# One input projection of a two-layer hybrid backbone: z and q computed in pieces of two row blocks by 512 columns

## The chip, the cores and the metric

The kernel runs on one core of one Trainium2 chip. TensorE (PE) multiplies, ScalarE (ACT), VectorE (DVE) and GpSimd (POOL) do the rest, SyncE (SP) issues the large loads; each takes its own instructions in order, and semaphores tie them together. The metric is the device time of one execution in microseconds. The kernel before took 1467.08 us (median of three runs, 1463.37 to 1467.37).

## The reference, cut to what matters

Two layers work on 256 latent tokens and 256 context tokens of 1024 features. Each layer projects the normed tokens by one matrix `w_in` and cuts the columns apart: k and v, x and B and dt of a state-space scan, C, q (512 columns), z (512 columns), and 1536 for a long convolution. z gates the scan, q goes into attention:

```python
h = _modulate(_rmsnorm(x, p['norm1_g']), sh1, sc1)
proj = h @ p['w_in']                                   # 1024 x 3856
...
q = _rope2d(_rmsnorm(_split_heads(proj[..., OFF_Q:OFF_Q + ATTN_INNER], ATTN_HEADS), p['q_norm_g']), rope) * ATTN_SCALE
...
y = y * jax.nn.silu(z.astype(F32))                     # z = proj[..., OFF_Z:OFF_Z + SSD_INNER]
y = _rmsnorm(y, p['ssd_norm_g'])
```

In the second layer (the last) the context tokens need neither z nor q, so these are computed for 256 tokens there and for 512 in the first.

## The kernel before, in words

Every product with a weight is computed as three float32r matmuls: high part of h by high part of w, high by low, low by high. The weights come in pieces of 128 partitions x 1024 numbers (512 KB) into a ring of four slots. A piece goes SP (load to `w_raw`), ACT (`round_w`, L1165, makes `w_hi`), DVE (`split_w`, L1467, makes `w_lo` over `w_raw`), PE. PE raises `w_used` when it is done with a piece, and SP waits for it before it loads the piece that is four further on into the same slot.

The projection takes 30 pieces per layer, in fifteen chunks of 256 columns and two pieces each (rows 0 to 511 of w_in, then 512 to 1023; the table `W_IN`). The order is four chunks `xbc` (pieces 0 to 7), two of `z` (8 to 11), `kv` (12, 13), two of `q` (14 to 17), six of `hy` (18 to 29). In the text "piece 8" is s = 8 of this count, in either layer.

Chunks xbc and hy are turned (features on partitions, moving operand h, up to 512 tokens wide, L595 to L597). Chunks z, kv and q have tokens on partitions: the stationary operand is a 128 x 128 block of h, the moving operand 256 columns of weights (L865 to L867). For each tile of 128 tokens PE runs through all eight blocks of rows, 24 matmuls, and so through both pieces; a tile takes half a PSUM bank. PE waits for both split pieces ahead of the first tile, and gives back both in the last tile: the first piece 12 matmuls before the second.

PSUM has eight banks. Banks 0 to 3 are two pairs, which chunks take in turn (`q % 2` of a running count, "pair 0" and "pair 1" here). `pair_open` makes PE wait until the pair's last reader has raised `pair_free`. z is read by ACT (Silu into `zs`, L1229), q by DVE (copy into `qk`, L1592), one chunk each, two tiles to an instruction. The other banks carry small work that is put between the pieces by hand: `at_piece(s)` ahead of a piece and `in_piece(s)` in its middle. There stand the spectra of the convolution's filter in layer 0 (`filter_spectrum`, L689, at pieces 9 to 11, copied by DVE at L1643), the scan (`cum_rows` L716 and L719, ACT's exponentials L1284, `y_head` L731; L823, L829), and the modulation rows of layer 0 (L534, L554). What ACT and DVE do in slot s is written out in the same way in two loops over s, in the order of their lines.

## Time and profile before

| what | value |
|---|---|
| three runs | 1467.37, 1467.08, 1463.37 us |
| the profiled execution | 1465.52 us, span 1463.7 us |
| granted TensorE clock over the span | 0.969 |
| PE busy | 1355.6 us (93%) |
| DVE busy, ACT busy | 695.9 us (48%), 525.1 us (36%) |
| projection of layer 0 | about 65 to 325 us of the span |
| projection of layer 1 | about 969 to 1124 us of the span |

The span runs from the first instruction to the last; 1.8 us of the profiled execution lie around it. The duration of a matmul in the rows holds its way through the array, so matmuls overlap; what one costs in a stream is read from start to start. In a timeline row the first number is the start, the second the time, and the bracket is how long the engine had been idle and what ended that.

### The profile page before, as it was taken

The page shows a single profiled execution, that of the slowest core. Times are in us where ns is not written, and L with a number is a line of the kernel's source. Part 1 is how long each engine was busy: PE and PEld are TensorE (multiplying, and loading weights), DVE is VectorE, ACT ScalarE, POOL GpSimd, SP SyncE. Part 2 cuts the span into 40 slices and gives each one's busy share as a digit, 9 for nine tenths or more (in the row PEclk, how much of TensorE's full clock was granted, in tenths as well). Part 3 has the DMA queues.
Part 4 walks back from the last instruction along what each step waited for, and adds up shares of the span by engine and source line. Part 5 has one row for each costly group of instructions (what it writes and reads, how often), then busy time and mean ns, then how long its engine had stood idle before and what let it go on. Part 6 is the DMA issues. An engine that isn't in the chain of part 4 may idle for free. (4 is left out here: it accounts for less than half of the span.)

```text
span 1463.7 us, 20023 instructions
## 1 busy us (share of the span) xinstructions
PE 1355.6 (93%) x8564; PEld 1093.0 (75%) x8564; DVE 695.9 (48%) x1134; ACT 525.1 (36%) x866; POOL 1.7 (0%) x8
## 2 busy tenths in 40 slices
PE   4799999998989889999999999999987889899997
PEld 2376778776657667777777788659876768899996
DVE  0544244755556663433222233364486555655554
ACT  4443333643031352222112232355464224544442
POOL 0000000000000000000000000000000000000000
PEclk9699999999999999999999999999999999999998
DMA  9553313442101215545555533313333203465652
GB/s 296 163 144 86 116 58 120 121 139 97 43 1 30 73 51 176 173 148 169 164 163 165 169 116 93 94 29 110 92 87 101 73 15 87 130 184 178 185 175 85
DMA packets 171216, 172.03 MB, mean 118 GB/s; under 512 B 9172, under 2 KB 169590, under 8 KB 171128
## 3 DMA queue, kind: packets, MB, share of 16 engines
q1 hardware_dynamic: 169284, 170.41, 38.2%
q8 instruction: 67, 1.10, 0.3%
q10 hardware_dynamic: 1844, 0.36, 0.1%
q14 instruction: 21, 0.17, 0.0%
HBM read 169.69 MB, written 1.05 MB: 117 GB/s over the span
## 5 line engine op out<-in xcount | busy, mean ns | idle before, releaser
L1467 DVE TENSOR_TENSOR w_lo<-w_raw,w_hi 128x1024 fp32r<-128x1024 f32 (+1 forms) x220 | 264.0, 1203 | 312.2 <-ACT w_hi L1165 311.4
L1165 ACT ACTIVATE w_hi<-w_raw 128x1024 fp32r<-128x1024 f32 (+1 forms) x220 | 228.3, 1042 | 396.6 <-DMA w_raw<-in_w_gu_dram 183.7
L595 PE MATMUL ps<-h_hi,w_hi 128*128 128x512 f32 (+1 forms) x960 | 340.0, 354 | 3.1 <-DVE w_lo L1467 2.5
L596 PE MATMUL ps<-h_lo,w_hi 128*128 128x512 f32 (+1 forms) x960 | 330.6, 344 | 0.0
L597 PE MATMUL ps<-h_hi,w_lo 128*128 128x512 f32 (+1 forms) x960 | 330.5, 344 | 0.0
L595 PEld LDWEIGHTS ps<-h_hi,w_hi 128*128 128x128 f32 x960 | 183.9, 192 | 43.0 <-issue 20.6
L595 PE MATMUL ps<-f_hi,w_hi 128*128 128x512 f32 (+1 forms) x544 | 191.2, 352 | 14.9 <-DVE xT L1773 5.3
L597 PEld LDWEIGHTS ps<-h_hi,w_lo 128*128 128x128 f32 x960 | 183.6, 191 | 22.2
L596 PEld LDWEIGHTS ps<-h_lo,w_hi 128*128 128x128 f32 x960 | 183.9, 192 | 19.5
L597 PE MATMUL ps<-f_hi,w_lo 128*128 128x512 f32 (+1 forms) x544 | 184.7, 339 | 0.0
L596 PE MATMUL ps<-f_lo,w_hi 128*128 128x512 f32 (+1 forms) x416 | 141.2, 340 | 0.0
L595 PEld LDWEIGHTS ps<-f_hi,w_hi 128*128 128x128 f32 x544 | 104.4, 192 | 33.3 <-issue 12.0
L597 PEld LDWEIGHTS ps<-f_hi,w_lo 128*128 128x128 f32 x544 | 104.6, 192 | 11.2
L596 PEld LDWEIGHTS ps<-f_lo,w_hi 128*128 128x128 f32 x416 | 80.2, 193 | 9.0 <-issue 1.0
L865 PE MATMUL ps<-w_hi,h_hi 128*128 128x256 f32 x256 | 77.6, 303 | 0.0
L866 PE MATMUL ps<-w_lo,h_hi 128*128 128x256 f32 x256 | 74.0, 289 | 0.0
L867 PE MATMUL ps<-w_hi,h_lo 128*128 128x256 f32 x256 | 73.9, 289 | 0.0
L865 PEld LDWEIGHTS ps<-w_hi,h_hi 128*128 128x128 f32 x256 | 50.7, 198 | 4.6 <-issue 4.4
L1330 ACT ACTIVATE probT<-ps 128x512 f32<-128x512 f32 (+1 forms) x48 | 22.6, 523 | 87.3 <-PE ps L944 87.3
L1502 DVE SCALAR_TENSOR_TENSOR xT<-ps,modv,xT 128x256 f32<-128x256 f32 x72 | 30.4, 477 | 48.6 <-PE ps L597 48.5
L866 PEld LDWEIGHTS ps<-w_lo,h_hi 128*128 128x128 f32 x256 | 50.8, 198 | 0.4 <-issue 0.2
L867 PEld LDWEIGHTS ps<-w_hi,h_lo 128*128 128x128 f32 x256 | 50.7, 198 | 0.0
(276 smaller groups left out, 1605.6 us busy)
## 6 DMA issues: line engine op xcount, KB each, us to landing
w_raw<-in_w_gu_dram SPq DMA_DIRECT2D x88, 512.0 KB, 3.6
w_raw<-in_w_in_dram SPq DMA_DIRECT2D x60, 512.0 KB, 4.1
w_raw<-in_w_down_dram SPq DMA_DIRECT2D x32, 512.0 KB, 3.4
m_raw<-in_w_mod_dram SPq DMA_DIRECT2D x30, 512.0 KB, 5.2
m_even<-in_w_mod_dram SPq DMA_DIRECT2D x13, 1024.0 KB, 6.2
m_odd<-in_w_mod_dram SPq DMA_DIRECT2D x12, 1024.0 KB, 6.3
m_first<-in_w_mod_dram SPq DMA_DIRECT2D x8, 1024.0 KB, 13.2
w_raw<-in_w_out_dram SPq DMA_DIRECT2D x16, 512.0 KB, 3.4
```

Source lines behind the costliest of these rows:

```text
L595: mm(o, w_hi[:, i % RING, w], hi[:, 0:n], start=first and k == 0, stop=False)
L596: mm(o, w_hi[:, i % RING, w], lo[:, 0:n], start=False, stop=False)
L597: last = mm(o, w_lo[:, i % RING, w], hi[:, 0:n], start=False, stop=final and k == nk - 1)
L865: mm(o, h_hi[:, b, tok], w_hi[:, (i + half) % RING, w], start=(b == 0), stop=False)
L866: mm(o, h_hi[:, b, tok], w_lo[:, (i + half) % RING, w], start=False, stop=False)
L867: last = mm(o, h_lo[:, b, tok], w_hi[:, (i + half) % RING, w], start=False, stop=(b == KD - 1))
L1165: A(w_hi[:, i % RING, w], w_raw[:, i % RING, w], ACT.Copy).then_inc(w_hi_done, 1)
L1330: p.sig(A(probT[:, i % 2, j, 0:keys], ps[:, 6 + j, 0:keys], ACT.Exp), "probs_ready")
L1467: TT(w_lo[:, i % RING, w], w_raw[:, i % RING, w], w_hi[:, i % RING, w].bitcast(F32), ALU.subtract).then_inc(w_lo_done, 1)
L1502: ins = STT(out=res, in0=ps[:, 2 * (q % 2) + jj, s * L:(s + 1) * L], scalar=modv[:, l, gate_blk + blk, s:s + 1], in1=res, op0=ALU.mult, op ...
```

## The change

z and q are no longer two chunks each of four row blocks by 256 columns, but one computation of 512 columns in four pieces of two row blocks. The size of a piece and the order of pieces stay. A matmul takes 512 columns, and each tile of tokens has a whole bank: with four tiles (layer 0) z or q fills both pairs, with two tiles (layer 1) one pair, while the other is only waited for and given back. PE runs through all tiles in each piece, waits for one piece at a time and gives back each at its own end. ACT reads all of z after the fourth piece, and DVE all of q. In the loads a row of 1 KB becomes one of 2 KB.

```diff
--- before.py
+++ after.py
@@ -430,6 +430,16 @@
                     .then_inc(wdt_full, 16)
 
             def load_in(l, s):
+                kind, col, idx = W_IN[s // 2]
+                if kind in ("z", "q"):
+
+                    i, k0 = PLAN[l, "in"][0] + s, 4 * idx + 2 * (s % 2)
+                    if i >= RING:
+                        sp.wait_ge(w_used, i - RING + 1)
+                    c0 = col - CW * idx
+                    sp.dma_start(w_raw[:, i % RING, :].rearrange("p (k n) -> p k n", n=2 * CW),
+                                 w_in[l].rearrange("(k p) n -> p k n", p=P)[:, k0:k0 + 2, c0:c0 + 2 * CW]).then_inc(w_full[i % RING], 16)
+                    return
                 col, k0 = W_IN[s // 2][1], 4 * (s % 2)
                 load_w(PLAN[l, "in"][0] + s, w_in[l].rearrange("(k p) n -> p k n", p=P)[:, k0:k0 + 4, col:col + CW], 4)
 
@@ -847,8 +857,32 @@
                             block_of(i + half, q, 0, 4, wide, h_blocks(half), half == 0, half == 1)
                             in_piece(s + half)
                             block_of(i + half, q, 1, 4, wide, h_blocks(half), half == 0, half == 1).then_inc(w_used, 1)
+                    elif kind in ("z", "q"):
+
+                        qa = q - idx
+                        for half in range(2):
+                            at_piece(s + half)
+                            pe.wait_ge(w_lo_done, i + half + 1)
+                            if (idx, half) == (0, 0):
+                                pair_open(qa)
+                            if (idx, half) == (0, 1) and tiles == 2:
+                                pair_open(qa + 1)
+                            for t in range(tiles):
+                                if (idx, half, t) == (0, 0, 2):
+                                    pair_open(qa + 1)
+                                if t == tiles // 2:
+                                    in_piece(s + half)
+                                o = ps[:, 2 * ((qa + t // 2) % 2) + t % 2, :]
+                                tok = slice(t * P, (t + 1) * P)
+                                for k in range(2):
+                                    b, w = 4 * idx + 2 * half + k, slice(2 * k * CW, 2 * (k + 1) * CW)
+                                    mm(o, h_hi[:, b, tok], w_hi[:, (i + half) % RING, w], start=(b == 0), stop=False)
+                                    mm(o, h_hi[:, b, tok], w_lo[:, (i + half) % RING, w], start=False, stop=False)
+                                    last = mm(o, h_lo[:, b, tok], w_hi[:, (i + half) % RING, w], start=False, stop=(b == KD - 1))
+                                if t == tiles - 1:
+                                    last.then_inc(w_used, 1)
                     else:
-                        count = 4 if kind == "kv" else tiles
+                        count = 4
                         for u in range(2 * count):
                             if u % count == 0:
                                 at_piece(s + u // count)
@@ -1223,12 +1257,14 @@
                                     wc, bc = V_HCW + 12 + blk, V_HCB + blk
                                 A(dst, ps[:, b + jj, 0:wide], ACT.Identity, scale=vecT[:, l, wc:wc + 1],
                                   bias=vecT[:, l, bc:bc + 1]).then_inc(conv_init, 1)
-                        if kind == "z":
+                        if kind == "z" and idx == 1:
                             act.wait_ge(w_used, g0 + 2 * ch + 2)
-                            for bb in range(tiles // 2):
-                                last = A(zs[:, 2 * bb:2 * bb + 2, idx * CW:(idx + 1) * CW],
-                                         ps[:, b + bb, :].rearrange("p (t n) -> p t n", t=2), ACT.Silu)
-                            last.then_inc(pair_free[q % 2], 1)
+                            for t in range(tiles):
+                                ins = A(zs[:, t, :], ps[:, 2 * ((q - 1 + t // 2) % 2) + t % 2, :], ACT.Silu)
+                                if t % 2 == 1:
+                                    ins.then_inc(pair_free[(q - 1 + t // 2) % 2], 1)
+                                elif tiles == 2:
+                                    ins.then_inc(pair_free[q % 2], 1)
                     if s < 30:
                         round_w(g0 + s + 2)
                     if s % 2 == 1 and s >= 3 and W_IN[(s - 3) // 2][0] == "xbc":
@@ -1581,17 +1617,23 @@
                                 v2 = slice(2 * (idx - 2), 2 * (idx - 2) + 2)
                                 p.sig(TT(hyv[:, v2, 0:n], hyv[:, v2, 0:n], x1t[:, :, 0:n], ALU.mult), "hyv_ready")
                         elif kind in ("kv", "q"):
-                            dve.wait_ge(w_used, g0 + 2 * ch + 2)
-                            for bb in range(2 if kind == "kv" else tiles // 2):
-                                src = ps[:, b + bb, :].rearrange("p (t n) -> p t n", t=2)
-                                tt = slice(2 * bb, 2 * bb + 2)
-                                if kind == "kv":
+                            if kind == "kv":
+                                dve.wait_ge(w_used, g0 + 2 * ch + 2)
+                                for bb in range(2):
+                                    src = ps[:, b + bb, :].rearrange("p (t n) -> p t n", t=2)
+                                    tt = slice(2 * bb, 2 * bb + 2)
                                     V.tensor_copy(v_nat[:, tt, :], src[:, :, 128:256])
                                     ins = V.tensor_copy(qk[:, tt, 512:QKW], src[:, :, 0:128])
-                                else:
-                                    ins = V.tensor_copy(qk[:, tt, idx * CW:(idx + 1) * CW], src)
-                            ins.then_inc(pair_free[q % 2], 1)
-                            if kind == "q" and idx == 1:
+                                ins.then_inc(pair_free[q % 2], 1)
+                            elif idx == 1:
+                                dve.wait_ge(w_used, g0 + 2 * ch + 2)
+                                for t in range(tiles):
+                                    ins = V.tensor_copy(qk[:, t, 0:512], ps[:, 2 * ((q - 1 + t // 2) % 2) + t % 2, :])
+                                    if t % 2 == 1:
+                                        ins.then_inc(pair_free[(q - 1 + t // 2) % 2], 1)
+                                    elif tiles == 2:
+                                        ins.then_inc(pair_free[q % 2], 1)
+                                dve.wait_ge(pair_free[(q - 1) % 2], (q - 1) // 2 + 1)
                                 dve.wait_ge(pair_free[q % 2], q // 2 + 1)
                                 p.sig(V.memset(rs40[:], 1.0), "qk_ready")
                     if S_HEAD < s <= S_HEAD + HEADS:
```

TensorE, layer 0, the middle of piece 8 (the first of z), before. L554 and L534 are small matmuls of the modulation rows (`turn_row`, `mod_rows`), and what is in brackets is what a row waits for:

```order
L866 MATMUL ps<-w_lo,h_hi 128x256
L867 MATMUL ps<-w_hi,h_lo 128x256
L554 MATMUL ps<-msel,m_row 128x2 [waits row_ready]
L554 MATMUL ps<-msel,m_row 128x2
L534 MATMUL ps<-m_raw,cact 32x256 [waits m_full0]
L534 MATMUL ps<-m_raw,cact 32x256 x3
```

The same place after (L880, L881 are the new L866, L867, and L564, L544 the new L554, L534):

```order
L880 MATMUL ps<-w_lo,h_hi 128x512
L881 MATMUL ps<-w_hi,h_lo 128x512
L564 MATMUL ps<-msel,m_row 128x2 [waits row_ready,pair_free1]
L564 MATMUL ps<-msel,m_row 128x2
L544 MATMUL ps<-m_raw,cact 32x256 [waits m_full0]
L544 MATMUL ps<-m_raw,cact 32x256 x3
```

A wait for pair 1 now stands in the middle of the piece, ahead of the small matmuls; before it stood ahead of piece 10.

ScalarE, layer 0, from the slot of piece 9's end to that of piece 12, before (`bnat` and `gT` belong to the scan; `w_hi` rows are `round_w` of pieces 12, 13 and 14):

```order
L1158 ACTIVATE m_row<-ps 128x256 [waits row_turned,m_used]
L1229 ACTIVATE zs<-ps 128x2x256 [waits w_used]
L1229 ACTIVATE zs<-ps 128x2x256
L1165 ACTIVATE w_hi<-w_raw 128x1024 [waits w_full0]
L1165 ACTIVATE w_hi<-w_raw 128x1024 [waits w_full1]
L1270 ACTIVATE gT<-ps 128x1024 [waits g_psum]
L1158 ACTIVATE m_row<-ps 128x256 [waits row_turned,m_used]
L1229 ACTIVATE zs<-ps 128x2x256 [waits w_used]
L1229 ACTIVATE zs<-ps 128x2x256
L1165 ACTIVATE w_hi<-w_raw 128x1024 [waits w_full2]
```

The same after (L1199 is `round_w`, L1263 reads z):

```order
L1192 ACTIVATE m_row<-ps 128x256 [waits row_turned,m_used]
L1199 ACTIVATE w_hi<-w_raw 128x1024 [waits w_full0]
L1199 ACTIVATE w_hi<-w_raw 128x1024 [waits w_full1]
L1306 ACTIVATE gT<-ps 128x1024 [waits g_psum]
L1192 ACTIVATE m_row<-ps 128x256 [waits row_turned,m_used]
L1263 ACTIVATE zs<-ps 128x512 [waits w_used]
L1263 ACTIVATE zs<-ps 128x512 x3
L1199 ACTIVATE w_hi<-w_raw 128x1024 [waits w_full2]
```

The two readings of the first z chunk have gone from ahead of `round_w` of piece 12 to behind the whole of z, where four stand in a row ahead of `round_w` of piece 14.

VectorE, layer 0, where the second q chunk ended, before (L1592 copies q, L1605 adds one head of the scan, L1467 is `split_w`):

```order
L1659 TENSOR_TENSOR xw<-xsn,wst 128x512
L1592 COPY qk<-ps 128x2x256 [waits w_used]
L1592 COPY qk<-ps 128x2x256
L1596 MEMSET rs_118 128x40 [waits pair_free0]
L1605 TENSOR_TENSOR ysum<-ysum,ps 128x4x64 [waits y_head_done,acc_read]
L1467 TENSOR_TENSOR w_lo<-w_raw,w_hi 128x1024 [waits w_hi_done]
```

The same after (L1631 copies q, L1647 and L1503 are the new L1605 and L1467):

```order
L1701 TENSOR_TENSOR xw<-xsn,wst 128x512
L1631 COPY qk<-ps 128x512 [waits w_used]
L1631 COPY qk<-ps 128x512 x3
L1638 MEMSET rs_118 128x40 [waits pair_free0,pair_free1]
L1647 TENSOR_TENSOR ysum<-ysum,ps 128x4x64 [waits y_head_done,acc_read]
L1503 TENSOR_TENSOR w_lo<-w_raw,w_hi 128x1024 [waits w_hi_done]
```

Four copies stand where two stood, and the marker behind them waits for both pairs.

## Rows read from the trace of the kernel before

**Rows 1.** The page: busy time by engine, and the chain that ended last, by engine.
```profile
PE 1355.6 (93%) x8564; PEld 1093.0 (75%) x8564; DVE 695.9 (48%) x1134; ACT 525.1 (36%) x866; POOL 1.7 (0%) x8
...
PE 18%; DVE 2%; ACT 1%; DMA 0%; issue 0%; DVEq 0%; ACTq 0%
```

**Rows 2.** Groups by form, the matmuls of 256 moving columns in z, kv and q.
```profile
L865 PE MATMUL ps<-w_hi,h_hi 128*128 128x256 f32 x256 | 77.6, 303 | 0.0
```

**Rows 3.** Timeline, TensorE: 24 matmuls of 256 columns, then what follows.
```profile
235.58 0.36 PE L865 MATMUL ps<-w_hi,h_hi 128*128 128x256 f32 x1
...
238.53 0.60 PE L823 MATMUL ps<-xw,bnat 128*128 128x256 f32 x2
```

**Rows 4.** Timeline, TensorE: 12 matmuls of 512 columns, then what follows.
```profile
257.21 0.48 PE L595 MATMUL ps<-h_hi,w_hi 128*128 128x512 f32 x1
...
260.05 0.38 PE L829 MATMUL ps<-st,xbc 128*128 128x256 f32 x1
```

**Rows 5.** Timelines, VectorE and TensorE, piece 8 of layer 0 and its end.
```profile
135.56 1.40 DVE L1576 SCALAR_TENSOR_TENSOR xbc<-ps,vecT,xbc 128x510 f32<-128x510 f32 x2
...
135.97 0.51 PE L554 MATMUL ps<-msel,m_row 128*128 128x2 f32 x4
...
141.06 0.68 DVE L1638 TENSOR_TENSOR t_sum<-t_sum,t_hyb 1x512 f32<-1x512 f32 x1
...
141.84 1.96 PE L689 MATMUL ps<-t_sum,c_fwd 128*128 128x512 f32 x4 [1.74 <-issue]
```

**Rows 6.** Timelines, SyncE, ScalarE, VectorE and TensorE, pieces 10 and 12 of layer 0.
```profile
151.49 0.37 SPq L384 DMA_DIRECT2D w_raw<-in_w_in_dram  x1
...
155.73 1.06 ACT L1165 ACTIVATE w_hi<-w_raw 128x1024 fp32r<-128x1024 f32 x1 [1.71 <-DMA w_raw<-in_w_in_dram]
...
156.82 1.22 DVE L1467 TENSOR_TENSOR w_lo<-w_raw,w_hi 128x1024 fp32r<-128x1024 f32 x1 [6.83 <-ACT w_hi L1165]
157.97 0.68 DVE L1643 COPY spec<-ps 128x512 f32<-128x512 f32 x1
...
157.21 0.28 PE L867 MATMUL ps<-w_hi,h_lo 128*128 128x256 f32 x1
158.71 1.98 PE L689 MATMUL ps<-t_diff,c_fwd 128*128 128x512 f32 x4 [1.22 <-DVE spec L1643]
```

**Rows 7.** Timelines, ScalarE and TensorE, the end of z and kv, layer 0.
```profile
174.71 1.09 ACT L1229 ACTIVATE zs<-ps 128x512 f32<-128x512 f32 x2 [2.65 <-PE ps L867]
177.84 1.06 ACT L1165 ACTIVATE w_hi<-w_raw 128x1024 fp32r<-128x1024 f32 x1 [2.05 <-DMA w_raw<-in_w_in_dram]
...
175.91 0.47 PE L865 MATMUL ps<-w_hi,h_hi 128*128 128x256 f32 x1
...
184.60 2.15 PE L716 MATMUL ps<-csT,c_sq 8*128 8x512 f32 x4 [1.51 <-ACT em L1284]
```

**Rows 8.** Timelines, ScalarE and TensorE, the same place in layer 1.
```profile
1028.33 0.60 ACT L1229 ACTIVATE zs<-ps 128x512 f32<-128x512 f32 x1 [0.70 <-PE ps L867]
1030.56 1.06 ACT L1165 ACTIVATE w_hi<-w_raw 128x1024 fp32r<-128x1024 f32 x1 [1.63 <-DMA w_raw<-in_w_in_dram]
...
1029.01 0.36 PE L865 MATMUL ps<-w_hi,h_hi 128*128 128x256 f32 x1
...
1035.95 1.21 PE L716 MATMUL ps<-csT,c_sq 8*128 8x256 f32 x4 [0.95 <-ACT em L1284]
```

**Rows 9.** Timelines, VectorE and TensorE, layer 1, the end of q.
```profile
1067.31 0.68 DVE L1592 COPY qk<-ps 128x512 f32<-128x512 f32 x1
...
1068.72 0.36 PE L595 MATMUL ps<-h_hi,w_hi 128*128 128x256 f32 x1
```

**Rows 10.** Windows: stretch, busy us (instructions) of PE, PEld, DVE, ACT, POOL, PEclk, DMA.
```profile
144.00:154.00 10.00, 10.00 (x70) 7.66 (x68) 1.22 (x2) 2.53 (x5) 0.00 (x0) 1.00 0.13 26
...
188.00:195.00 7.00, 7.00 (x35) 7.00 (x34) 2.69 (x3) 1.28 (x5) 0.00 (x0) 0.51 0.01 2
...
1038.00:1042.00 4.00, 4.00 (x22) 4.00 (x22) 2.02 (x3) 0.56 (x3) 0.00 (x0) 0.58 0.00 0
```

## The prediction

> **What bounds the kernel now.** I read the page first. PE is busy 93% of the span, the next engine 48% [rows 1]. The chain that ended last is followed back for a fifth of the span only, and in that part PE has 18 points of 21 [rows 1], so it says what the end hangs on but not where z and q stand. Busy shares hide what matters here, since a matmul's time in the rows overlaps with its neighbours'. So I went on to the groups by form, to count what is replaced, and then to the timelines of the two projections, engine by engine, to see where PE stops and for whom. There the reader is to see PE streaming almost without a break, with a few stops of 1 to 2 us. Where PE streams, only what shortens the stream counts. Where it stops, only what shortens the chain that releases it counts. Last come the windows, for the granted clock.
>
> **What is replaced.** The 256-column form stands 256 times on each of three lines, 768 matmuls [rows 2]. Of these kv keeps 4 tiles x 8 blocks x 2 layers = 64 per line. z and q have 192 per line, 576 in all, and become 288 of 512 columns. In blocks of 24 old or 12 new matmuls (one tile's worth) that is 24 blocks: 16 in layer 0 (four tiles, four chunks) and 8 in layer 1.
>
> *The stream.* A block of 24 narrow matmuls behind `y_head` takes from 235.58 to 238.53, 2.95 us [rows 3]. Twelve wide ones in the same surroundings, also behind `y_head`, take from 257.21 to 260.05, 2.84 us [rows 4]. Both multiply the same number of columns at full clock; the shapes turn round (weights move, h is loaded), but the tile sizes are the same. The difference is 0.11 us a block, 24 x 0.11 = 2.6 us. Bounds: nothing, if the wide form costs more with weights as the moving operand, and twice that, 5.3 us, as what I allow above. I take 2.6. The Trainium skill ("TensorE: Matmul & The Clock Gate", Back-to-back issue gap) gives a gap of N/2.4 + 2.5 ns; by it a pair of narrow matmuls would lose only the one fixed 2.5 ns, an estimate of 288 x 2.5 ns = 0.7 us, and the whole sum below would be 1.9 us smaller. The rows show 123 ns a narrow matmul against that page's 109, and 237 ns a wide one against its 216, so it does not fit here and the measurement decides.
>
> *A new wait inside piece 8, layer 0.* z now needs both pairs of banks at once. Pair 1 is released by DVE's last work on the fourth xbc chunk, which ends at 136.96 [rows 5]. PE reaches the small matmuls in the middle of the piece at 135.97 now [rows 5], and would wait there about 1.0 us. Queued behind it are those small matmuls and the rest of the piece. But at the end of the piece PE stands until 141.84 for a chain on DVE that ends at 141.74 (L1638) [rows 5], and nothing in that chain waits for PE. PE has been idle for 1.74 us by then [rows 5], from 140.1. So the wait fits into an existing stop, at no cost, with 0.7 us to spare. The 0.22 us that the stream gains in this piece are lost in the same stop. If the cover weren't there, 1.0 us would be.
>
> *The stop at 158.71, layer 0.* Here PE waits for a copy on DVE (L1643), 1.4 us more than the 0.12 us that follow a narrow matmul [rows 6]. That copy stands behind `split_w` of piece 12 (156.82), that behind `round_w` (155.73), and that behind a load issued at 151.49, since PE gives back piece 8 only in the last tile [rows 6]. In the new order piece 8 is given back at its own end, some 10 us earlier, at about 141; the load needs 4.2 us (151.49 to 155.73), and ACT is no longer held by z's first half ahead of `round_w`, only by a modulation row in the middle of piece 9. Piece 8 comes back 12 matmuls of 0.12 us ahead of the end of piece 9, so that end is at 152.9 and the middle a block earlier, at about 150. With 1.06 and 1.22 us for `round_w` and `split_w` the piece is split by about 153. PE needs the copy at 157.3, and the copy's own input is there a block earlier, at about 154.4. The stop goes: 1.4 us. What is late next is the copy itself (0.68 us), still 2 us ahead of PE's need. Bounds 0 and 1.4.
>
> *The head of kv, layer 0.* Now kv needs pair 0, which ACT frees with the second of four readings that start after all of z. Two such readings took 1.09 us from 174.71, so pair 0 is free at about 175.8; kv begins at 175.91, since `cum_rows` stands ahead of it [rows 7]. Nothing, or 0.1 us.
>
> *The stop at 184.60, layer 0.* PE waits 1.5 us for the exponentials on ACT [rows 7]. ACT's chain from the end of z: two readings (1.09), then 2.05 us idle for the load of piece 14, then `round_w`, eight scalings, a table load, the exponentials [rows 7]. The load is now early, since piece 10 comes back in the middle of z's second half; in place of the 2.05 us stand two more readings, 1.0 us. The chain is 1.0 us shorter and the stop shrinks by that. Bounds: the burst could cost its 1.0 us with the wait for the load left as it is (-1.0), or take off the whole 1.5.
>
> *The same in layer 1.* One reading more (0.5 us) against 1.63 us idle: the chain shortens by 1.1, and the stop at 1035.95 is 0.95 to 1.0 us [rows 8]. But kv must now wait for the second reading, until about 1029.45 instead of 1029.01 [rows 8], so 0.45 us go to this wait and 0.55 us are left.
>
> *The end of q.* In layer 1 DVE has one copy more ahead of the pair that hy takes: 1067.31 + 0.6 + 0.68 = 1068.6, against hy's start at 1068.72 [rows 9]. Put down 0.1 us, at most 0.7 if DVE comes late. In layer 0 two copies more stand where DVE waits for PE anyway.
>
> *Loads.* Bytes and pieces are equal, rows twice as long. No stop of PE between 133 and 246 us waits for a load itself but through the two chains above, so I put nothing beside them.
>
> **The sum.** 2.6 - 0.2 + 1.4 - 0.1 + 1.0 + 0.55 - 0.1 = 5.2 us, rounded. Against its own profiled execution, 1465.52 us (span 1463.7 and 1.8 around it), that is **1460.3 us**. That execution lies 1.6 us under the median of the three runs, and inside their spread, so against 1467.08 the change looks like 6.8 us, 0.46%. Downstream nothing gives it back that I see, as the later stops of both projections hang on work that starts from PE.
>
> **The rivals.**
>
> *The clock gives more (1455.6 us).* Behind both shrunk stops the granted clock was at the lower level, 1.2 GHz: 0.51 over 188 to 195 and 0.58 over 1038 to 1042, after PE had stopped and then run the short matmuls of the scan [rows 10]. The first cost 7.0 x 0.49 = 3.4 us and the second 1.7, of which 3.0 and 1.6 fall on matmuls. If PE, busier there, keeps 2.4 GHz, both come on top: 5.2 + 4.6 = 9.8. Against it: the short matmuls stay, and part of the first stop. The same page (What's actually happening) says that the clock follows how busy PE has been; it would be this rival.
>
> *Only the stream (1463.1 us).* The three stops have another cause than the profile's last releaser, for instance PE's own scan matmuls, or loads that come no sooner because they share the queue with the modulation weights. Then 2.4 us are left. For it: every load of a piece in layer 0 has such a neighbour. Against it: these neighbours already run without delay today.
>
> *Nothing arrives (1464.7 us).* The wide matmul with moving weights costs as two narrow ones, and of the 2.95 us that the stops give, new waits of 1.0, 0.45 and 0.7 us at the bank pairs take all but 0.8.
>
> *Slower (1470.1 us).* One mechanism: the waits for bank pairs, at the middle of piece 8, at the head of kv and at the head of hy, drop the clock to 1.2 GHz. Today PE holds 1.00 over 144 to 154 in spite of the 1.7 us ahead of it [rows 10]. Split in two stops with little work between, that could fall. A block at the lower level costs about 2.3 us more (7.0 x 0.49 over 1.5 blocks), three such blocks 7.0; with the stream's 2.4 and no shorter stops that is +4.6. It decides from about three lowered blocks on.
>
> **How the numbers follow.** The forecast has 0.45, the clock 0.20, only the stream 0.18, nothing 0.10, slower 0.07. The time is the forecast's. Its own range is 1458 to 1463; the range for 8 in 10 reaches down to the clock's case and up past "nothing", 1455.5 to 1466.5. What a measurement of this kernel can tell from no change is about 0.3%, 4.4 us, so faster begins at 1462.7 and slower at 1471.5, against the median. Most of the forecast's case, all of the clock's and a little of the stream's are faster: 0.64. Same has 0.30, slower 0.06.
>
> **What would show it.** Blocks of twelve wide matmuls in z and q take 2.84 us. PE idles about 1 us at the middle of piece 8 for pair 1, and again less than 1 us ahead of L689. The second stop for L689 is gone, and `w_hi` of piece 12 is made some 4 us earlier relative to the end of piece 9. PE's stop ahead of the second `cum_rows` is about 0.5 us in layer 0 and none in layer 1, where kv starts 0.5 us later behind z. It would be wrong if wide blocks take 2.95 us, if ACT still idles for piece 14 behind its readings, or if the granted clock falls in stretches where it is 1.00 today.

## The result, and the profile after

The changed kernel takes 1459.41 us (median of 10 runs, 1452.69 to 1462.56), the kernel before on the same chip 1467.19 us (median of 10, 1463.36 to 1472.34). The ratio is 0.9945, with a 95% interval of 0.9926 to 0.9964: 7.8 us less. The profiled execution took 1460.89 us (span 1459.1), the one of before 1465.52.

The page of the changed kernel, answering to [rows 1] and [rows 2]. A group's row ends in busy us, mean ns of one, and idle time before it:

```profile
PE 1352.5 (93%) x8276; PEld 1076.2 (74%) x8276; DVE 695.2 (48%) x1134; ACT 525.5 (36%) x866; POOL 1.7 (0%) x8
...
PE 17%; DVE 2%; ACT 1%; DMA 0%; issue 0%; DVEq 0%; ACTq 0%
...
L879 PE MATMUL ps<-w_hi,h_hi 128*128 128x512 f32 x96 | 40.3, 420 | 0.0
```

288 matmuls are gone (8564 to 8276), as counted, and 96 of the wide form stand on each of three lines. Neither the shares nor the chain tell where 8 us came from; the stops and the stretches do.

The timelines of the changed kernel in layer 0, SyncE, ScalarE, VectorE and TensorE, answering to [rows 3], [rows 5], [rows 6] and [rows 7]:

```profile
136.17 0.39 PE L881 MATMUL ps<-w_hi,h_lo 128*128 128x512 f32 x1
137.61 0.61 PE L564 MATMUL ps<-msel,m_row 128*128 128x2 f32 x4 [1.05 <-DVE xbc L1612]
142.43 1.96 PE L699 MATMUL ps<-t_sum,c_fwd 128*128 128x512 f32 x4 [0.70 <-issue]
...
141.76 0.37 SPq L384 DMA_DIRECT2D w_raw<-in_w_in_dram  x1
150.64 1.05 ACT L1199 ACTIVATE w_hi<-w_raw 128x1024 fp32r<-128x1024 f32 x1
151.73 1.23 DVE L1503 TENSOR_TENSOR w_lo<-w_raw,w_hi 128x1024 fp32r<-128x1024 f32 x1 [1.27 <-ACT w_hi L1199]
155.02 0.69 DVE L1685 COPY spec<-ps 128x512 f32<-128x512 f32 x1 [2.06 <-PE ps L699]
157.36 0.39 PE L881 MATMUL ps<-w_hi,h_lo 128*128 128x512 f32 x1
157.59 1.88 PE L699 MATMUL ps<-t_diff,c_fwd 128*128 128x512 f32 x4
...
173.17 2.07 ACT L1263 ACTIVATE zs<-ps 128x512 f32<-128x512 f32 x4 [2.54 <-PE ps L881]
175.09 1.08 ACT L1199 ACTIVATE w_hi<-w_raw 128x1024 fp32r<-128x1024 f32 x1
176.04 3.31 ACT L1311 ACTIVATE ysum<-xsn,bc 128x256 f32<-128x256 f32 x8
180.66 2.17 ACT L1320 ACTIVATE em<-ps,bia 128x128 f32<-128x128 f32 x8
174.40 0.45 PE L899 MATMUL ps<-w_hi,h_hi 128*128 128x256 f32 x1
181.85 2.15 PE L726 MATMUL ps<-csT,c_sq 8*128 8x512 f32 x4 [0.30 <-ACT em L1320]
...
210.76 0.48 PE L879 MATMUL ps<-w_hi,h_hi 128*128 128x512 f32 x1
213.60 0.59 PE L839 MATMUL ps<-st,xbc 128*128 128x256 f32 x2
```

The reader is to see five things. The stop of 1.74 us ahead of the first L689 is now two, 1.05 in the middle of the piece and 0.70 at its end. The load for piece 12 is issued at 141.76 instead of 151.49, ACT rounds it at 150.64 instead of 155.73, and the copy of L1685 is back to waiting for PE: the stop at 158.71 is gone (157.36 to 157.59 is one matmul). ACT goes from its four readings into `round_w` of piece 14 with no gap, where it had idled 2.05 us. The stop ahead of the second `cum_rows` has shrunk from 1.51 to 0.30. And a block of twelve takes 2.84 us.

In layer 1 the same timelines, answering to [rows 8] and [rows 9], after:

```profile
1028.53 1.08 ACT L1263 ACTIVATE zs<-ps 128x512 f32<-128x512 f32 x2 [1.07 <-PE ps L881]
1029.50 1.06 ACT L1199 ACTIVATE w_hi<-w_raw 128x1024 fp32r<-128x1024 f32 x1
...
1029.76 0.36 PE L899 MATMUL ps<-w_hi,h_hi 128*128 128x256 f32 x1 [0.31 <-ACT zs L1263]
1035.67 0.70 PE L726 MATMUL ps<-csT,c_sq 8*128 8x256 f32 x4
1066.08 0.36 PE L605 MATMUL ps<-h_hi,w_hi 128*128 128x256 f32 x1
```

kv waits for the second reading, 0.31 us, and `cum_rows` waits for nobody.

*Where the time went.* I cut the execution at the first matmul of z and the first of hy. The stretch from z to hy has one length, to 0.2 us, in both profiles of each kernel that was profiled twice, which makes it a finer measure than the total:

| stretch | before | after | difference |
|---|---|---|---|
| start to z, layer 0 | 133.10 | 133.68 | +0.6 |
| z to hy, layer 0 | 113.23 | 109.02 | -4.2 |
| hy, layer 0, to z, layer 1 | 768.51 | 772.92 | +4.4 |
| z to hy, layer 1 | 53.88 | 50.46 | -3.4 |
| hy, layer 1, to the end | 394.98 | 393.02 | -2.0 |

So the changed part gained 7.6 us, and 4.4 us were lost in a stretch where no instruction of the program differs. The 2.0 us of the last row belong to the execution: profiled again, the changed kernel takes 395.05 us there, as long as before. Windows (stretch, busy us and instructions of PE, PEld, DVE, ACT, POOL; granted clock; DMA share, GB/s) of that stretch in the kernel before:

```profile
246.33:1014.84 768.51, 738.55 (x4020) 564.03 (x4020) 351.02 (x573) 247.42 (x395) 0.75 (x2) 0.99 0.36 111
348.50:351.90 3.40, 3.40 (x10) 2.63 (x9) 0.00 (x0) 0.87 (x2) 0.00 (x0) 0.50 0.00 0
499.30:502.70 3.40, 2.28 (x10) 1.91 (x11) 3.40 (x6) 0.00 (x0) 0.00 (x0) 1.00 0.63 159
533.40:540.30 6.90, 5.15 (x16) 4.13 (x17) 6.20 (x15) 4.84 (x10) 0.00 (x0) 0.75 0.01 4
```

And of the changed kernel, with the stretch behind the second `cum_rows` of layer 0 and that of layer 1:

```profile
242.70:1015.62 772.92, 742.38 (x4020) 567.02 (x4020) 350.71 (x573) 245.57 (x388) 0.75 (x2) 0.99 0.35 109
342.30:349.10 6.80, 5.69 (x18) 4.86 (x19) 1.44 (x7) 2.48 (x3) 0.00 (x0) 0.50 0.04 13
499.30:502.70 3.40, 3.40 (x9) 2.63 (x8) 1.52 (x2) 0.00 (x0) 0.00 (x0) 0.50 0.00 1
533.40:540.30 6.90, 6.13 (x15) 4.81 (x16) 6.65 (x16) 4.84 (x10) 0.00 (x0) 0.51 0.00 1
...
185.30:192.10 6.80, 6.80 (x34) 6.80 (x34) 2.69 (x3) 1.23 (x5) 0.00 (x0) 0.50 0.01 2
1034.00:1038.00 4.00, 4.00 (x34) 3.52 (x33) 1.05 (x3) 3.43 (x10) 0.00 (x0) 1.00 0.00 0
```

Both have 4020 matmuls there. The clock is at the lower of its two levels, 1.2 GHz, for 6.8 + 3.4 + 6.9 = 17.1 us near 342, 499 and 533 in the changed kernel. Before has 3.4 near 348 and 3.4 near 536 (half of the last window, 0.75), so the changed kernel has 10.3 us more, at half speed worth at most 5.1, since PE is idle for part of them. Behind the second `cum_rows` the fall of layer 0 (0.51 over 188 to 195 in [rows 10]) has stayed; that of layer 1 (0.58 over 1038 to 1042) is gone.

### The profile page after: what moved, and what is told of

The parts are those of the page before. It is cut to its first block and busy times, and to the rows that moved or that the text cites. A ratio compares the mean times of both kernels' runs of the same rounds, so it can differ in the third digit from the quotient of the medians.

```text
span 1459.1 us, 19448 instructions
## 1 busy us (share of the span) xinstructions
PE 1352.5 (93%) x8276; PEld 1076.2 (74%) x8276; DVE 695.2 (48%) x1134; ACT 525.5 (36%) x866; POOL 1.7 (0%) x8
## 3 DMA queue, kind: packets, MB, share of 16 engines
HBM read 169.69 MB, written 1.05 MB: 117 GB/s over the span
## 5 line engine op out<-in xcount | busy, mean ns | idle before, releaser
L1503 DVE TENSOR_TENSOR w_lo<-w_raw,w_hi 128x1024 fp32r<-128x1024 f32 (+1 forms) x220 | 263.8, 1203 | 302.0 <-ACT w_hi L1199 301.5
L1199 ACT ACTIVATE w_hi<-w_raw 128x1024 fp32r<-128x1024 f32 (+1 forms) x220 | 228.5, 1042 | 376.2 <-DMA w_raw<-in_w_gu_dram 185.9
L1937 DVE TENSOR_TENSOR hidden<-gate,ps 128x1024 f32<-128x1024 f32 (+1 forms) x22 | 21.0, 953 | 56.9 <-PE ps L607 56.7
L1849 DVE TENSOR_REDUCE sm<-ps 128x2 f32<-128x1024 f32 (+1 forms) x24 | 25.1, 1045 | 45.4 <-PE ps L960 45.3
L1150 ACT ACTIVATE sqr<-xT 128x512 f32<-128x512 f32 (+1 forms) x40 | 20.0, 540 | 73.7 <-DVE xT L1538 40.8
L879 PE MATMUL ps<-w_hi,h_hi 128*128 128x512 f32 x96 | 40.3, 420 | 0.0
L1320 ACT ACTIVATE em<-ps,bia 128x128 f32<-128x128 f32 x96 | 26.4, 377 | 31.3 <-PE ps L729 31.2
L881 PE MATMUL ps<-w_hi,h_lo 128*128 128x512 f32 x96 | 37.6, 392 | 0.0
```

The source lines that it names most:

```text
L879: mm(o, h_hi[:, b, tok], w_hi[:, (i + half) % RING, w], start=(b == 0), stop=False)
L881: last = mm(o, h_lo[:, b, tok], w_hi[:, (i + half) % RING, w], start=False, stop=(b == KD - 1))
L1199: A(w_hi[:, i % RING, w], w_raw[:, i % RING, w], ACT.Copy).then_inc(w_hi_done, 1)
L1320: ins = A(em[:, 2 * (h % 2) + d, t * P:(t + 1) * P], ps[:, 6 + d, t * P:(t + 1) * P], ACT.Exp, bias=bia[:, t, d * 8 + h:d * 8 + h + 1])
L1503: TT(w_lo[:, i % RING, w], w_raw[:, i % RING, w], w_hi[:, i % RING, w].bitcast(F32), ALU.subtract).then_inc(w_lo_done, 1)
L1849: p.chain(V.tensor_reduce(out=sm[:, 0, 2 * (i % 4):2 * (i % 4) + 2], in_=ps[:, 4:6, 0:T if i // 4 < 2 else L], op=ALU.max, axis=AX_X, nega ...
```

## The experiments

*Theory A*: the gain is what the prediction's terms say, a denser stream and two chains that release PE earlier, and the small matmuls' new wait costs nothing. *Theory B*: the shorter stops matter through the clock. What is left over, the 4.4 us lost downstream, is either the luck of one profile or belongs to the kernel.

**The changed kernel again**, unchanged, five rounds.

> The changed kernel once more, unaltered. Theory A (what z and q gain is the same in every execution, what is left is where the granted clock falls): from the start of z to the start of hy PE needs 109.0 us in layer 0 as in its first profile (133.68 to 242.70), within 0.1 us, unless a fall of the clock lies there; the low-clock stretches between 325 and 969 us, where nothing was changed, stand elsewhere or are another number; over the timed runs time follows the mean granted clock, about 1 us per 0.001. Theory B (the new order itself costs clock further on): the same two stretches of 6.8 us at 342 and 533 us and the one at 499 us come back.

It took 1459.55 us (6 runs, 1455.55 to 1463.79) against 1468.11 of before, ratio 0.9941 (0.992 to 0.9962). The stretches from z to hy are 109.06 and 50.45 us. Windows of its profile:

```profile
182.20:189.10 6.90, 6.90 (x34) 6.90 (x34) 2.69 (x3) 1.67 (x7) 0.00 (x0) 0.51 0.01 2
240.07:1012.40 772.33, 742.06 (x4021) 566.92 (x4021) 350.75 (x573) 245.51 (x388) 0.75 (x2) 0.99 0.35 109
339.20:346.10 6.90, 5.30 (x17) 4.56 (x18) 1.92 (x7) 2.48 (x3) 0.00 (x0) 0.51 0.11 38
```

The falls came back at the same places of the program (this execution reached z 2.7 us earlier, and they stand 3 us earlier), in the changed part and downstream of it up to z of layer 1. Where I had expected them to stand elsewhere in a second execution, I was wrong. Behind hy of layer 1 they did not all come back: the mean granted clock is 0.92 over 1081 to 1253 us, where the first profile has 0.95 over the same part of the program, 1084 to 1256.

**Pieces given back late.** Both pieces of a pair are released at the end of the second, as before the change (the next to last tile for the first, the last for the second).

```diff
-                                if t == tiles - 1:
+                                if half == 1 and t >= tiles - 2:
                                     last.then_inc(w_used, 1)
```

> The changed kernel, but PE gives back both pieces of z and of q only near the end of every second piece: six wide matmuls ahead of it and at it, as before the change. Matmuls, banks, readings and their places stay. Theory A (the early return of pieces removes the stop for the second L689 and shortens the one ahead of the second cum_rows): the stop of 1.4 us comes back in layer 0, the stop ahead of the second cum_rows grows from 0.4 to about 1.5 us in layer 0 (ACT is held for its load again, its two more readings lie in that time) and from 0 to about 0.6 in layer 1; together 3 us slower than the changed kernel. Rival B (the stops went because ACT no longer reads the first z chunk ahead of round_w, and because the stream is shorter): both stops stay gone, no difference over 0.5 us.

1461.38 us (12 runs), ratio 0.9969 (0.995 to 0.9987). z to hy takes 111.29 us (+2.3 against after) and 51.60 (+1.2): 3.4 us, where the prediction's terms for the stops were 1.4 + 1.0 + 0.55 = 3.0. Its timelines, layer 0:

```profile
153.54 1.06 ACT L1199 ACTIVATE w_hi<-w_raw 128x1024 fp32r<-128x1024 f32 x1 [5.34 <-DMA w_raw<-in_w_in_dram]
154.63 1.23 DVE L1503 TENSOR_TENSOR w_lo<-w_raw,w_hi 128x1024 fp32r<-128x1024 f32 x1 [6.72 <-ACT w_hi L1199]
155.78 0.68 DVE L1685 COPY spec<-ps 128x512 f32<-128x512 f32 x1
156.51 1.98 PE L699 MATMUL ps<-t_diff,c_fwd 128*128 128x512 f32 x4 [1.31 <-DVE spec L1685]
...
181.55 2.15 PE L726 MATMUL ps<-csT,c_sq 8*128 8x512 f32 x4 [0.98 <-ACT em L1320]
```

ACT again waits for the load, DVE's copy again stands behind `split_w`, and PE's stop of [rows 6] is back, 1.31 us. The early release is what had removed it. The stop ahead of `cum_rows` was expected to grow to 1.5 us in layer 0 and 0.6 in layer 1, and grew to 0.98 and 0.57. Theory A holds for the stops. By the total alone it could not be told, since the intervals of this kernel and the changed one overlap.

**Narrow matmuls.** The old loads and pieces (four row blocks by 256 columns) and 256-column matmuls, with the new banks, release and readings.

The edit of the loads, which only takes out the new branch of `load_in`, is left out here:

```diff
...
-                                for k in range(2):
-                                    b, w = 4 * idx + 2 * half + k, slice(2 * k * CW, 2 * (k + 1) * CW)
+                                o = o[:, idx * CW:(idx + 1) * CW]
+                                for k in range(4):
+                                    b, w = 4 * half + k, slice(k * CW, (k + 1) * CW)
```

> The changed kernel with its banks, early return and late readings, but the old pieces (four row blocks by 256 columns) and matmuls of 256 columns: 576 narrow ones in place of 288 wide. Theory A (the wide form streams better by 0.11 us a block of 12): blocks take 2.95 in place of 2.84 us, 24 blocks, 2.6 us slower than the changed kernel, with the stops as in the changed one (the 0.2 us of the first two blocks lost in the stop for L689). Rival B (a matmul pair costs the same either way, by the page's gap formula 2.5 ns a pair): 0.7 us or less.

1460.54 us (12 runs), ratio 0.9954 (0.9936 to 0.9972). z to hy takes 110.62 (+1.6) and 51.35 us (+0.9). A block of 24 in its timeline:

```profile
203.51 0.36 PE L870 MATMUL ps<-w_hi,h_hi 128*128 128x256 f32 x1
...
206.47 1.03 PE L823 MATMUL ps<-xw,bnat 128*128 128x256 f32 x4
```

2.96 us against 2.84. The stream gives 2.5 us in 24 blocks, as taken (2.6, less 0.2 that fell into a stop), and not the 0.7 us that was estimated from the Trainium skill's figure for an isolated matmul ("TensorE: Matmul & The Clock Gate", Back-to-back issue gap). The row decided rightly here. By the total alone this could not be told, since the intervals of this kernel and the changed one overlap.

Of the 7.6 us, this leaves 7.6 - 3.4 - 2.5 = 1.7 us that neither experiment took back, if the two can be added. Most of it, 1.3 us, lies in layer 1. The clock's fall of layer 1 fits it: 3.4 us at the lower level (1038.0 to 1041.4 before) are worth 1.7, and neither of the two kernels has them. No run took this fall back alone.

**The scalings of ysum moved**, to see whether the rest of the stop at `cum_rows` and the fall behind it hang together. ACT makes eight scalings (3.31 us, L1311 above) between `round_w` of piece 14 and the exponentials. They need only `xsn` and stood in slot 12. First variant: behind `gT` in slot 11, in both layers. Without their condition they run under the one of `gT`:

```diff
                     if s == S_G:
                         p.after("g_psum")
                         p.sig(A(gT[:, :, 0:tiles, :], ps[:, 6:8, 0:n].rearrange("p g (t s) -> p g t s", s=P), ACT.Copy), "gT_ready")
-                    if s == S_HEAD:
                         p.own("xsn_ready")
                         for h in range(HEADS):
```

> The changed kernel with ACT's eight scalings (ysum from xsn, 3.3 us in layer 0, 2.4 in layer 1) moved one slot up, from behind the readings of z to behind gT, where ACT idles. Theory A (ACT's chain from the end of z decides the stop ahead of the second cum_rows, and the stop goes before the fall of the clock): the chain is 3.3 us shorter, the stop of 0.4 us in layer 0 goes; if the fall to 1.2 GHz behind it (185 to 192 us) hangs on that stop, it goes too and 3 us more are gained, 3.4 in all. Rival B (the fall comes from the short matmuls of the scan): only the 0.4 us, the fall stays within some us of its place.

1454.87 us (6 runs, 1452.53 to 1456.98), ratio 0.9911 (0.9893 to 0.993). Layer 0: 104.57 us, 4.5 under the changed kernel; no stop is left ahead of the second `cum_rows`, and no fall behind it. Layer 1: 52.98 us, 2.5 over. There the scalings stand ahead of the readings of z, kv waits for these, and the clock falls; this loss had not been expected. Timeline of TensorE in layer 1:

```profile
1021.42 0.36 PE L899 MATMUL ps<-w_hi,h_hi 128*128 128x256 f32 x1 [1.35 <-ACT zs L1263]
...
1022.21 0.40 PE L899 MATMUL ps<-w_hi,h_hi 128*128 128x256 f32 x1
1022.40 0.41 PE L900 MATMUL ps<-w_lo,h_hi 128*128 128x256 f32 x1
```

Here the fall is seen from matmul to matmul: from start to start they take 0.12 us in a stream at 2.4 GHz, and 0.21 behind 1022.2, 0.8 us after a stop of 1.35.

**The scalings in slot 10**, behind `round_w` of piece 12, in both layers, where ACT has nothing due.

```diff
                     if s < 30:
                         round_w(g0 + s + 2)
+                    if s == S_B + 1:
+                        p.own("xsn_ready")
+                        for h in range(HEADS):
+                            hd = slice(h * HD, (h + 1) * HD)
+                            ins = A(ysum[:, 0:tiles, hd], xsn[:, 0:tiles, hd], ACT.Copy, scale=bc16[:, l, 2, h:h + 1])
+                        p.sig(ins, "ysum_init")
...
```

The same lines are taken out of slot 12.

> The changed kernel with ACT's eight scalings in slot 10 in both layers, behind round_w of piece 12 and ahead of that of piece 13, so that they delay neither z's readings nor gT. In the run with the scalings one slot up, layer 1 lost 2.5 us (kv waited 1.5 us for the readings, and the clock fell behind that). Theory A: layer 0 as in that run (104.6 us from z to hy, no fall of the clock there), layer 1 as in the changed kernel (50.4 us) since nothing there waits for ACT but kv for the second reading: 1452.5 us, 2.5 under the run before it. Rival B: layer 1 keeps the loss, because the fall of the clock there comes from elsewhere: 1455 us.

1453.66 us (6 runs, 1450.84 to 1457.16) against 1465.29 of before (11 runs), ratio 0.9926 (0.9912 to 0.9939). z to hy: 104.58 and 50.45 us. This is the best version, with 4.4 us less than the changed kernel from z to hy in layer 0. Windows of both layers:

```profile
174.00:196.00 22.00, 22.00 (x161) 18.14 (x161) 10.97 (x16) 10.26 (x29) 0.00 (x0) 1.00 0.35 113
1018.00:1042.00 24.00, 23.69 (x168) 20.26 (x167) 12.39 (x19) 10.53 (x22) 0.00 (x0) 1.00 0.28 82
```

The clock stays at the full level. And the second `cum_rows` of layer 0 in its timeline, against the row at 181.85 of the changed kernel:

```profile
178.59 1.13 PE L726 MATMUL ps<-csT,c_sq 8*128 8x512 f32 x4
```

No idle time ahead of it, and 1.13 us instead of 2.15 for the same four matmuls. The longer row hides a second wait: `cum_rows` waits for the exponentials once for each direction, and ACT makes these one behind the other (2.17 us for both, from 180.66 to 182.83). A narrow cut of the changed kernel's timeline, 182.99 to 183.30, shows the first matmul of the second half alone:

```profile
182.88 0.69 PE L726 MATMUL ps<-csT,c_sq 8*128 8x512 f32 x1
```

It starts 0.05 us behind the end of the exponentials and 1.03 us behind the first half. With the scalings in slot 10 both halves start together, at 178.59. So what went is 0.30 us of idle time, 1.0 us inside the row, and the fall of 6.8 us at half speed, 3.4 us; that makes 4.7, and 4.4 were measured. Theory B is right in this: the stop and the wait in the row had cost 1.3 us, less than half of what followed them.

**The small matmuls ahead of the wait for pair 1**, in the middle of piece 8.

```diff
-                                if (idx, half, t) == (0, 0, 2):
-                                    pair_open(qa + 1)
                                 if t == tiles // 2:
                                     in_piece(s + half)
+                                if (idx, half, t) == (0, 0, 2):
+                                    pair_open(qa + 1)
```

> The changed kernel with the small modulation matmuls of piece 8 in layer 0 ahead of PE's wait for pair 1 instead of behind it. Theory A (this wait lies within a stop that a chain on DVE ends): PE waits 0.2 to 0.4 us for the pair in place of 1.3, and the whole difference of 1.0 us is added to the stop ahead of the first L689, which then takes about 2 us; z to hy in layer 0 stays 109.0 us. Rival B (the wait is on the path): 108.0 us.

One execution, 1456.65 us; z to hy 109.04 and 50.45 us, nothing gained there. Its timeline:

```profile
136.00 0.50 PE L564 MATMUL ps<-msel,m_row 128*128 128x2 f32 x4
...
142.02 1.96 PE L699 MATMUL ps<-t_sum,c_fwd 128*128 128x512 f32 x4 [1.80 <-issue]
```

Without the 1.05 us in the middle the stop at the end is 1.80 instead of 0.70, and L699 starts 8.75 us after z in both, as it did before the change (8.74). The wait was covered, as predicted. The single time of 1456.65 lies within the changed kernel's runs and says nothing beside that.

**The kernel before, with the scalings in slot 10.** The same edit on the old order.

> The kernel before, with nothing altered but the scalings, moved to slot 10 behind round_w of piece 12. Theory A (the second cum_rows waits for ACT's chain from the end of z, and the stop brings the fall of the clock behind it): the stops of 1.5 us in layer 0 and 1.0 in layer 1 go, and with them the falls at 188 to 195 and 1038 to 1041 (3.0 and 1.6 us): 7 us faster than before, 0.5%; the stop of 1.4 us ahead of the fourth L689 grows by up to nothing, since round_w of piece 12 stands ahead of the scalings. Rival B (the falls come from the short matmuls): 2.5 us, falls in place.

1460.32 us (6 runs, 1456.89 to 1462.15), ratio 0.9964 (0.995 to 0.9978). z to hy takes 107.97 us (-5.3 against before) and 51.56 (-2.3). In its timeline two of the old stops stand untouched:

```profile
142.22 1.95 PE L689 MATMUL ps<-t_sum,c_fwd 128*128 128x512 f32 x4 [1.75 <-issue]
...
158.98 1.98 PE L689 MATMUL ps<-t_diff,c_fwd 128*128 128x512 f32 x4 [1.11 <-DVE spec L1643]
```

Behind the first the clock stays at 1.00, as in [rows 10]. But the third stop, and the falls behind it in both layers, are gone; in layer 1 a new stop of 0.67 us stands ahead of the first `cum_rows`, since `gT` now comes later on ACT. This edit of one place is worth as much from z to hy (7.6 us) as the whole change, and most of that is clock.

The total gives only 5.0 us, where 7 had been expected. From hy of layer 0 to z of layer 1 this kernel takes 5.1 us more than before:

```profile
241.45:1015.07 773.62, 743.73 (x4021) 568.06 (x4020) 351.08 (x573) 247.59 (x395) 0.76 (x2) 0.98 0.36 110
```

The clock is at the lower level for 6.8, 3.4 and 6.8 us near 342, 499 and 533, as in the changed kernel, and for 3.4 us near 287. So the loss downstream comes also where z and q are computed in the old way.

**Both edits on the changed kernel** (scalings in slot 10, small matmuls first).

> Both edits on the changed kernel: scalings in slot 10, small matmuls of piece 8 ahead of the wait for pair 1. As the second edit only moves idle time within one piece, it should take the time of the run with the scalings alone, 1452.5 us, within 1 us, and 14 us less than before. Rival: the smaller idle time within piece 8 lets the clock fall less often there, up to 2 us more.

1455.46 us (5 runs, 1453.68 to 1457.57), ratio 0.9932 (0.9919 to 0.9946); z to hy 104.58 and 50.45 us. That is 9.8 us under before, where 14 had been expected, and 1.8 above the kernel with the scalings alone, with intervals that overlap. The second edit adds nothing to the first.

**The kernel before again**, one profile, for the 4.4 us lost downstream.

> The kernel before, unchanged, profiled a second time. Question: in the changed kernel 4.8 us were lost between 321 and 1015 us, where no instruction differs, at three low-clock stretches (near 342, 499 and 533 us; before had two shorter ones near 348 and 536). Theory F (the stretches belong to the kernel: its earlier part sets them): this profile again has two stretches of 3.4 us near 348.5 and 536.2 and none at 499, mean granted clock 0.93 over 330 to 355, 1.00 over 490 to 510, 0.93 over 520 to 545, and z to hy takes 113.2 us in layer 0 and 53.9 in layer 1 with the falls behind both second cum_rows. Theory V (they vary from one execution to the next and the changed kernel's gain is not given back there): 0.86, 0.91 and 0.86 over the three stretches, as in the changed kernel, with z to hy still at 113.2 and 53.9.

1464.47 us. z to hy takes 113.07 and 53.98 us, and the windows of its profile are those of the first one:

```profile
244.38:1012.64 768.26, 738.41 (x4020) 564.07 (x4020) 351.08 (x573) 247.59 (x395) 0.75 (x2) 0.99 0.36 111
346.50:349.90 3.40, 3.40 (x10) 2.63 (x9) 0.00 (x0) 0.91 (x2) 0.00 (x0) 0.50 0.00 0
492.00:504.00 12.00, 9.50 (x43) 7.56 (x42) 9.08 (x14) 4.24 (x6) 0.00 (x0) 1.00 0.37 110
```

768.51 and 768.26 us twice for before, 772.92 and 772.33 twice for after. In these four profiles the loss of some 4 us (3.8 to 4.7, each against each) belongs to the kernel, not to the execution.

**The scalings behind gT again**, one profile.

> The kernel with the scalings behind gT in both layers, unchanged, profiled a second time. Its first profile had the pattern of the kernel before downstream (0.93, 1.00, 0.93 over 330 to 355, 490 to 510, 520 to 545), although its layer 0 up to the start of hy took the same 104.6 us as the kernel with the scalings in slot 10, which has 0.86, 0.91, 0.86. Theory F (the kernel sets them): the same 0.93, 1.00, 0.93 again. Theory V (they vary between executions): 0.86, 0.91, 0.86. In both the wait of 1.6 us at the head of kv of layer 1 and the fall behind it, 0.86 over 1018 to 1030, come back.

1459.03 us. z to hy takes 104.58 and 53.11 us, and kv's wait in layer 1 and the fall behind it came back. Downstream the mean clock was 0.93, 0.91 and 0.93 over the three stretches, where the first profile had 0.93, 1.00 and 0.93. The fall near 492 was new, one of 3.4 us near 282 in the first profile was gone, and the one near 340 stood 3.5 us nearer to z; that near 530 stood at the same distance from z. The stretch from hy of layer 0 to z of layer 1 took 770.39 and 770.13 us, between before and the changed kernel.

## Why the prediction was right, and where its sum was not

The forecast was 1460.3 us, inside 1455.5 to 1466.5; 1459.41 was measured. Against the median it had promised 6.8 us, and 7.8 were found; but of the 6.8 the sum gave only 5.2, and 1.6 came from taking one profiled execution as the base, so that the time fits as closely as this is in part luck. By its steps, with what was measured from z to hy:

- *The stream*, 2.6 - 0.2: right. Putting the narrow matmuls back cost 2.5 us, and the block is 2.84 us long.
- *The wait in piece 8*, nothing: right. It waits 1.05 us, the stop behind it shrinks by the same, and taking the wait away gains nothing.
- *The stop at 158.71*, 1.4: right, and by the chain that was named. The piece was split by 152.96, where "about 153" was forecast, and the copy ended at 155.71, 1.9 us ahead of PE's need. `w_hi` of piece 12 came 5.4 us earlier relative to the end of piece 9, not "some 4": at 150.64 with that end at 153.29, against 155.73 and 152.93.
- *The stop at 184.60*, 1.0: right in kind, somewhat too small, 1.2 us.
- *kv and `cum_rows` in layer 1*, 0.55: kv waits 0.31 us where 0.45 were given, and the stop ahead of `cum_rows` is gone.
- *The end of q*, 0.1: right. In layer 1 hy starts 0.92 us behind the start of the last scan matmuls, 0.1 more than before the change.

Together these terms measure 2.5 + 3.4 = 5.9 us against 5.2. What the sum lacked is clock, twice and with opposite signs. First, the rival "the clock gives more" (1455.6 us there, 1455.7 by its own terms) came half true. Its place in layer 1 gave 1.7 us, as it had priced it; its place in layer 0 gave nothing, since 0.30 us of the stop, and the wait inside `cum_rows`, were left. The prediction gave this case 0.20 as one event for both places, and they should have been two. Second, the step "downstream nothing gives it back that I see" failed. It looked at waits only, and there it was right: between hy of layer 0 and z of layer 1 PE stands idle for 30.0 us before and 30.5 after (768.51 - 738.55, 772.92 - 742.38). But the clock was at the lower level for 10.3 us more there, in three stretches, and the whole took 4.4 us longer. The prediction had named this as what would make it wrong ("if the granted clock falls in stretches where it is 1.00 today") and priced it only inside z and q, at the bank pairs. None fell there; they fell 100 to 300 us further on.

In the profiled executions the gain is therefore 4.6 us, 7.6 from z to hy and 3.0 given back, nearly the forecast's 5.2, but by errors that cancel, which is luck. And 2.0 of the 4.6 lie behind hy of layer 1, where the changed kernel's second profile showed no gain. Over all runs it is 7.8 us. Most of the difference goes with the clock: both profiled executions of before (1465.52 and 1464.47 us) lie 2.6 and 3.6 us under the median of its 23 runs, 1468.11, and had 0.969 and 0.970 of the full clock where those have a median of 0.967. At the 1.1 us per 0.001 found below for the changed kernel, that is 2 to 3 us. Why most executions of before had less is not known, since there is no trace of them.

What stays open is why the clock falls near 342, 499 and 533. The stretches contain the same instructions in both kernels. It isn't the new z and q alone: all ten profiles of the eight altered kernels take longer than before (768.3 and 768.5 us) from hy of layer 0 to z of layer 1, 770.1 to 774.7 us, the one with the old z and q among them at 773.6. It isn't the shift alone: the two variants with the scalings moved run layer 0 from z to hy in the same 104.6 us, and have 0.86, 0.91, 0.86 in one case and 0.93, 1.00 (or 0.91), 0.93 in the other. No experiment here changed that part of the program.

## What to carry to other kernels

Price a stop by what the clock does behind it, not only by its length: read the granted clock of the ten microseconds after every stop, and where it is at half, ask which instruction in the chain of the late engine could be done earlier. When a ring piece is given back decides how early the next is ready, so releasing at the piece's own end can remove stops two engines away. Compare two kernels by the stretch between two landmarks of the program as well as by the total: here that separated terms of 1 to 3 us, which totals that spread over 10 us did not.

## What the hardware showed that I had not expected

- *Total time follows the granted clock.* Of the changed kernel's ten runs the slowest, 1462.56 us, had a mean granted clock of 0.966 and the fastest, 1452.69, of 0.975: 1.1 us per 0.001. The stretches from z to hy were within 0.2 us in two profiles of each of three kernels, so in these profiles the spread lies elsewhere: the two of the changed kernel differ by 2.7 us ahead of z and by 2.0 us behind hy of layer 1.
- *The length of a stop alone does not decide whether the clock falls.* A stop of 1.74 us ahead of 512-column matmuls left it at 1.00 [rows 5, 10]. One of 0.30 us ahead of `cum_rows` of layer 0, with the wait inside it, was followed by 6.8 us at 1.2 GHz, as was each longer one at that place (seven profiles), and none of the four kernels without that stop had the fall. In layer 1, with 256 columns instead of 512 in `cum_rows`, 0.95 and 1.10 us, in the two profiles of before, were followed by 3.4 us, and the smaller stop of the late release, 0.57 us, by none. Which property of these matmuls matters, their 8 rows or the short ones behind them, no run tested apart; with the stop gone the same matmuls ran at 1.00.
- *A row of several matmuls can hide a wait.* The four of `cum_rows` take 1.13 us where both halves are free to start and 2.15 where the second waits; the idle time shown is only that ahead of the first. In layer 1 they took 1.21 before [rows 8] and 0.70 after, 0.5 us that the prediction's term for this stop did not contain.
- *Many falls repeat, not all.* The Trainium skill ("TensorE: Matmul & The Clock Gate", HAM oscillation) describes a kernel in which each wait for data brings the lower clock back, every time; its waits are of 3 to 5 us, for loads. The fall behind the stop of layer 0 came back every time too, but behind waits of 0.29 to 1.57 us, for ScalarE. The same page (What's actually happening) says that the number of slow matmuls at a kernel's start varies between runs, and over the first 130 us the mean granted clock does vary here, 0.87 and 0.89 in two profiles of before, 0.87 and 0.92 in two of after. From z of layer 0 to z of layer 1 the falls of before and of the changed kernel came back in a second profile at the same distance from z, to 0.5 us. In the kernel with the scalings behind `gT` they did not all: the first profile has falls 150 and 208 us behind z, the second 205 and 358, and both one at 396. Nor did all those behind hy of layer 1 in the changed kernel.
